# Casting the weights from DRAM to DRAM ahead of use, in a two-layer Mamba-2 and attention kernel

## The reference

```python
# layer 1
x = x + mamba2_mixer(rms_norm(x, a_norm), a_in_proj, ..., a_out_proj)   # SSD, 32 heads, 8 groups
x = x + conv_ffn(x, f_norm[0], f_w_in[0], ..., f_w_down[0])             # gated, width-3 conv
# shared K/V, then layer 2
k, v = split(rms_norm(x, kv_norm) @ w_kv + b_kv)                        # k normed, rotary
q = rotary(rms_norm((rms_norm(x, b_norm) @ w_q + b_q), q_norm))
x = x + sliding_window_sink_attention(q, k, v, sinks) @ w_o + b_o       # window 128
x = x + conv_ffn(x, f_norm[1], f_w_in[1], ..., f_w_down[1])
```

## Time and profile before

| | us |
|---|---|
| median of 3 runs | 2031.58 (2028.68 to 2034.41) |
| the profiled execution, its own time | 2035.03 |
| span of its slowest core, which the profile shows (core 3) | 2034.0 |
| spans of the 8 cores | 2000.2 to 2034.0 |
| PE busy | 1850.5 (91% of the span) |
| DVE, ACT, POOL busy | 1393.1, 1191.9, 204.5 |

### The profile page before, as it was taken

How to read it: one execution, slowest core, us unless ns; L and a number is a source line. 1 busy time by engine, 2 the same in 40 slices (tenths; PEclk the granted TensorE clock), 3 DMA queues, 4 the chain that set the end, 5 groups by cost and what they waited for, 6 DMA issues and landing times.

```text
span 2034.0 us, 34214 instructions; the slowest of 8 cores (2000.2 to 2034.0 us)
## 1 busy us (share of the span) xinstructions
PE 1850.5 (91%) x10024; PEld 823.4 (40%) x10024; DVE 1393.1 (68%) x2384; ACT 1191.9 (59%) x2140; POOL 204.5 (10%) x325
## 2 busy tenths in 40 slices
PE   5787798989888899999999999999999998989999
PEld 3333343434433343444443444444443344433344
DVE  6787477977666675587785776688776656774362
ACT  4688556756767464556577665576476643665330
POOL 1122001122120011000101000000102000020000
PEclk9889899999899999999999999999999999999999
DMA  9879778978556999945432544644423343443344
GB/s 221 195 175 214 188 150 199 211 186 218 144 156 154 221 210 216 280 151 151 156 116 76 162 162 158 203 154 139 148 84 104 128 154 118 145 125 104 118 152 156
DMA packets 111062, 330.59 MB, mean 163 GB/s; under 512 B 14752, under 2 KB 33312, under 8 KB 110880
## 3 DMA queue, kind: packets, MB, share of 16 engines
q1 hardware_dynamic: 95184, 271.56, 40.7%
q0 software_dynamic: 15696, 56.83, 18.1%
HBM read 318.78 MB, written 66.39 MB: 189 GB/s over the span
## 4 chain that ended last, share of the span: by engine, by line
PE 74%; DMA 11%; ACT 5%; issue 5%; DVE 4%; SPq 1%; POOL 0%; DVEq 0%; ACTq 0%; POOLq 0%
PE ps_ps L353 67%; PE ps_ps L366 6%; DMA sb_ring_fw<-w 5%; PE ps_ps L373 2%; DMA sb_ring_mw<-w 2%; DMA w<-sb_ring_fw 1%; DMA al_scr<-sb_AHl 1%; ACT sb_facc L391 1%; DMA sb_SL<-as_scr 1%; DMA sb_facc<-pos 1%; DVE sb_macc L417 1%; SPq L429 1%; DVE sb_uF L406 1%; ACT sb_macc L391 1%; DVE sb_hF L406 0%
## 5 line engine op out<-in xcount | busy, mean ns | idle before, releaser
L353 PE MATMUL ps_ps<-sb_hF,sb_ring_fw 128*128 128x512 bf16 x2464 | 578.8, 382 | 16.0 <-DMA sb_ring_fw<-w 9.7
L353 PE MATMUL ps_ps<-sb_hM,sb_ring_mw 128*128 128x512 bf16 (+1 forms) x1568 | 395.0, 389 | 24.6 <-DVE sb_macc L417 9.1
L353 PE MATMUL ps_ps<-sb_ring_fw,sb_uF 128*128 128x512 bf16 (+1 forms) x1696 | 394.8, 376 | 11.2 <-DVE sb_uF L406 4.6
L353 PEld LDWEIGHTS ps_ps<-sb_hF,sb_ring_fw 128*128 128x128 bf16 x2464 | 235.7, 98 | 298.6 <-issue 37.7
L417 DVE SCALAR_TENSOR_TENSOR sb_facc<-ps_ps,sb_cst,sb_facc 128x511 f32<-128x511 f32 (+2 forms) x400 | 295.9, 745 | 18.3 <-PE ps_ps L353 1.4
L391 ACT ACTIVATE sb_facc<-ps_ps,sb_cst 128x512 f32<-128x512 f32 x213 | 162.7, 766 | 167.8 <-PE ps_ps L353 156.1
L417 DVE SCALAR_TENSOR_TENSOR sb_macc<-ps_ps,sb_cst,sb_macc 128x511 f32<-128x511 f32 (+1 forms) x336 | 247.6, 743 | 12.7 <-PE ps_ps L353 1.4
L353 PEld LDWEIGHTS ps_ps<-sb_ring_fw,sb_uF 128*128 128x128 bf16 x1696 | 158.1, 98 | 202.9 <-issue 42.0
L353 PEld LDWEIGHTS ps_ps<-sb_hM,sb_ring_mw 128*128 128x128 bf16 (+1 forms) x1568 | 149.6, 100 | 205.0 <-issue 56.3
L406 DVE TENSOR_TENSOR sb_xR<-sb_xR,ps_ps 128x512 f32<-128x512 f32 x128 | 86.6, 684 | 122.9 <-PE ps_ps L353 121.4
L353 PE MATMUL ps_ps<-sb_ring_mw,sb_ybuf 128*128 128x512 bf16 (+1 forms) x608 | 156.1, 388 | 15.5 <-DMA sb_ring_mw<-w 10.3
(11 more groups left out here) (219 smaller groups left out, 2309.0 us busy)
## 6 DMA issues: line engine op xcount, KB each, us to landing
sb_ring_fw<-w SPq DMA_DIRECT2D x218, 512.0 KB, 3.8
sb_ring_mw<-w SPq DMA_DIRECT2D x106, 512.0 KB, 5.0
sb_ring_fw<-w POOLq DMA_DIRECT2D x76, 512.0 KB, 9.8
w<-sb_ring_fw SPq DMA_DIRECT2D x76, 512.0 KB, 8.7
sb_ring_mw<-w POOLq DMA_DIRECT2D x32, 512.0 KB, 9.5
w<-sb_ring_mw SPq DMA_DIRECT2D x32, 512.0 KB, 8.0
sb_Er<-er_scr SPq DMA_DIRECT2D x28, 512.0 KB, 8.2
sb_xR<-x SPq DMA_DIRECT2D x16, 512.0 KB, 7.8
```

The costliest lines, as they stand in the source:

```text
L353: return self.add("pe", lambda e: e.matmul(out, lhsT, rhs, start=start, stop=stop), [lhsT, rhs] + ([] if start else [out]), [out], cost=ma ...
```

## The change

The class `Caster` is new. `ahead(tile)` issues, on POOL's queue, DMAs that cast whole tiles from `w32` to `w16`, from DRAM to DRAM, up to a limit that grows with the tile that is in use: 2 tiles ahead at first, one more for every third tile, 12 at most. Each waits for the last matmul that was emitted before it. The rings then load those tiles on SP from `w16` the first time too, after the cast of the tile has landed. The first 11 tiles are still cast on their way into the ring and written back. The gates of the other ring's first four casts go, since these casts are gone.

```diff
+class Caster:
+    def __init__(self, K, w32, w16, first, depth):
+        self.K, self.w32, self.w16 = K, w32, w16
+        self.first, self.depth, self.next = first, depth, first
+        self.gate = None
+        self.done = {}
+
+    def ahead(self, tile):
+        lim = min(NTILE, tile + 1 + min(self.depth, 2 + tile // 3))
+        pe = self.K.ops["pe"]
+        while self.next < lim:
+            j = self.next
+            o = self.K.dma("pool", self.w16[j], self.w32[j], f"cast{j % (self.depth + 2)}")
+            g = pe[-1] if pe and tile else self.gate
+            if g is not None:
+                o.deps.append(g)
+                g.signal = True
+            o.signal = True
+            self.done[j] = o
+            self.next += 1
 class Ring:
...
-            if first:
+            if first and tile < self.caster.first:
                 n = 768 if tile == 0 else SLOT
                 o = self.K.dma("pool", self.buf[:, slot, 0:n], self.w32[tile][:, 0:n], f"{self.name}c{slot}")
...
             else:
+                if tile >= self.caster.next:
+                    self.caster.ahead(tile)
                 n = 768 if tile == 0 else SLOT
                 o = self.K.dma("sp", self.buf[:, slot, 0:n], self.w16[tile][:, 0:n], f"{self.name}{slot}")
                 o.deps.append(self.written[tile])
...
+        if first:
+            self.caster.ahead(tile)
         if first and tile not in self.written:
...
-    written = {}
-    mring = Ring(K, "mw", 4, w32_d, w16_d, written)
-    fring = Ring(K, "fw", 4, w32_d, w16_d, written)
+    caster = Caster(K, w32_d, w16_d, 11, 12)
+    mring = Ring(K, "mw", 4, w32_d, w16_d, caster)
+    fring = Ring(K, "fw", 4, w32_d, w16_d, caster)
...
-                        fring.gate[g - 4] = last
```

More of the change, by code:

```diff
@@ L609, in run, with __init__ @@
         self.drain()
+class Caster:
[17 more added lines that the diff above has]
+            self.next += 1
 class Ring:
-    def __init__(self, K, name, nslot, w32, w16, written):
+    def __init__(self, K, name, nslot, w32, w16, caster):
         self.K = K
@@ L621, in __init__ @@
         self.nslot = nslot
-        self.w32, self.w16, self.written = w32, w16, written
+        self.w32, self.w16, self.caster, self.written = w32, w16, caster, caster.done
         self.buf = K.sb("ring_" + name, [128, nslot, SLOT], BF16)
@@ L844, in build @@
         mring.gate[j] = last
+    caster.gate = last
     K.dma("sp", cf[:], cf_d, "c2")
```

## The result

The change makes the kernel slower: 2152.9 us median of 4 runs (2149.73 to 2158.45) against 2031.32 for the kernel before beside it; ratio 1.0601, 95% interval 1.0573 to 1.0629. The forecast was 1998 us. The profiled execution took 2149.73 us, its span is 2148.7 us (core 3). In the runs `e6_fine` to `e9_late` and `e12_oneplan` to `e14_late12` one die ran slower than the other, in the kernel before too, so their times, and those of two runs compared with them, are the median span of the other die's four cores, marked "die", beside the same median of the kernel before.

The account below looks back on a forecast made before the run. TensorE bounds 1127 to 1471 us; only the first 860 us, where weights first come in, can change. Terms -21 - 3.6 - 5 - 3.7 - 5.7 + 5 = -34 take 2035.0 to 2001, 1998 us as median; range 1975 to 2032.

Parts of the forecast that it names:

- a slot is refilled by a plain load (3.8 us median to landing) and not by a cast (9.8 us): Rings: a freed slot has some 15 us until its next tile is due, so plain loads remove 13.8 us of waits.
- Crowding: Broadcast rows and positions land later beside more DMA work, +5 us; as rival "Crowding eats half", 2021 us, chance 0.20.
- The price of a cast: DMA engines: a DRAM-to-DRAM cast costs 3.4 to 5.0 us of 16 engines, taken as 4 us.
- the bytes' reckoning: DMA engines: for 98 tiles a plain load replaces a write-back of equal bytes, 1.6 us of 16 engines a tile.
- slower: the DMA engines become the bound: Rival, from tile 11 to the last cast: at 6 us a cast the engines are overfull, 2138 us; chance 0.15.
- over 5.3 us a cast: DMA engines: the cast price above which the slower rival's casts cost more than the 34 us won.
- casts may lag up to 12 tiles before anyone waits: Look-ahead of casts: the argument given against the rival that crowding eats half the gain.
- The waits on SP: SP's queue, first two stretches: without write-backs, `al_scr` is issued earlier, -3.6 us, and the positions, -5 us.
- The waits for the mixer ring: Ring waits, taken whole: -3.7 us for the mixer ring, -5.7 us in the out-projection of block 0.
- 18 was expected: SP's waits: the terms 3.6, 5, 3.7 and 5.7 us, 18 us in all, mostly winnable by order alone.
- the two places that I named: SP's queue: the `al_scr` write issued at 289.00 and the positions load at 423.64, both behind write-backs awaiting casts.
- The round of block 1: Second ConvFFN's first pass, in-projection: costs 23.9 us over block 2's round, of which 21 is won, -21 us.

Follow-up runs that it names:

- e6_fine: Changed kernel with each cast issued as four DMAs of 512 columns, pieces of 1 KB: die 2101.1 against 2017.7 us.
- e9_late: Kernel before, only the list schedule told that casts land 6 us later: die 2007.5 against 2017.7 us.
- e12_oneplan: e3_one with the list schedule told that casts land 6 us later: die 2419.9 against 2015.5 us.
- e14_late12: Kernel before, only the list schedule told that casts land 12 us later: die 2028.7 against 2015.5 us.
- e5_small: Kernel before plus 22 unneeded DRAM-to-DRAM casts in 4 KB pieces beside block 2's first ConvFFN: die 2060.1 against 2018.6 us.
- e3_one: Changed kernel, each cast waiting on POOL until the one before it has landed: 2127.45 us, ratio 1.0457 to the kernel before.
- e10_late5: Kernel before, only the list schedule told that casts land 6 us later (e9_late again): 2021.22 us, ratio 0.9932.
- e11_pace: Kernel before with e10_late5's order plus 12 paced DRAM-to-DRAM casts for the second ConvFFN: 2019.11 us, ratio 0.992.
- e4_big: Kernel before plus 22 unneeded DRAM-to-DRAM casts in 32 KB pieces beside block 2's first ConvFFN: die 2056.2 against 2018.6 us.
- e15_onedve: e3_one with POOL's elementwise work moved to DVE: 2134.8 us, ratio 1.0469 to the kernel before.
- e7_dumpfine: Kernel before plus 22 unneeded DRAM-to-DRAM casts in 1 KB pieces beside block 2's first ConvFFN: die 2048.9 against 2017.7 us.

## Why the prediction was wrong

**The step that failed** is "a slot is refilled by a plain load (3.8 us median to landing) and not by a cast (9.8 us)", with "Crowding" beside it, +5 us. 3.8 us is the landing of loads over the whole span, most of them with little beside them on POOL's queue; the same trace had 6.4 us for the mixer ring's 28 plain loads before 520 us, beside casts. I priced crowding by the share of busy DMA time, 1.1 us for a tenth, a slope from rows that stood beside 1.1 to 1.4 casts on the mean. What counts is what is queued on the other queue at that moment. Before, casts were held back by the four slots that they fill; the changed kernel issues up to 12 tiles ahead, with nothing to hold them back but a matmul, and up to 6 are in flight at once. 20.3 us of landing is more than the some 15 us that a ring covers, and PE waited 74.8 us.

The kernel before had the turns the right way round: what was urgent, the cast, stood in POOL's queue and landed in 9.8 us; what stood in SP's, the write-back, took 8.7 us but is read only a block later. The change puts what is urgent into the queue that got 28.5% of the engines' time beside 69.4% (`e5_small`), and look-ahead into the other.

**The price of a cast** was right (4 taken, 3.9 found in the queue), and so was the bytes' reckoning. The rival "slower: the DMA engines become the bound" came within 15 us of the time, 2138 against 2153, by luck: its condition, over 5.3 us a cast, wasn't met, and after the first stretch the share is 0.60 to 0.84. In the first stretch, with 0.93, the trace after looks like it; what tells them apart is `e3_one`, where the same bytes leave PE 2.1 us of waits for the mixer ring there. The argument against the rivals, "casts may lag up to 12 tiles before anyone waits", was true of SP (26 us) and beside the point.

**The waits on SP** for casts (-3.6, -5) were taken away: SP had 105.9 us of them from 256 to 512 us and none from 315 to 608 us after. But `al_scr` then took 20.5 us to land where it took 8.3, and the positions 18.5 where they took 14.7. The waits for the mixer ring (-3.7, -5.7) gave way to longer ones, 74.8 us for it in the first stretch and 11.1 us for the second ring from 608 to 736 us. That some of this can be won is shown by `e10_late5`: about 14 us, where 18 was expected; its gain lies in the mixer of block 0, with a higher clock, more than at the two places that I named.

**The round of block 1** (-21) became +14. The term was also too large by itself: 23.9 us is the difference on core 3. Over the eight cores of the same trace the round of block 1 takes 353.1 to 368.7 us, median 361.0, and the round of block 2 344.1 to 346.2, so the first pass cost the median core some 16 us. With 12 of its 33 tiles loaded plain, `e11_pace` won some 7 us of the round against `e10_late5`, by the eight cores' medians; what all 33 would give isn't shown.

**What is shown and what stays open.** Shown: the casts' queue delays the loads (`e3_one`, 20.3 to 5.2 us; `e4_big`, casts without any user), and with one cast in flight they come too late (`e15_onedve`). At most one in flight costs 4.6%, two 3.9%, up to 12 tiles ahead 6.0%: none of them is free, and a first use now needs two transfers, one after the other (7.5 and 5.2 us in `e3_one`), where one did before. How the some 90 us that `e3_one` loses divide between late casts, products on POOL and a lower clock isn't settled. Whether the urgent loads would fare better on another engine's queue than SP's wasn't tried.

## What to carry to other kernels

A transfer that is moved off the path still stands beside those that stay on it: price a load by its landing beside a full queue, not by a median over the span, and ask which queue holds what is needed next. Look-ahead must be held back by something, but with one transfer in flight at a time its latency can become the bound: in `e3_one` casts end to end were 55% of the chain from 60 to 700 us. Before a first use is split into two transfers, see whether what is to be won isn't to be had by the order of the issues alone. And read a term off several cores: the slowest one's 23.9 us was 16 on the median core.

## What the runs showed of the hardware

- A cast of 1 MB of float32 from DRAM to DRAM landed in 7.5 us (`e3_one`) and cost 2.9 us of 16 engines (`e15_onedve`, an estimate) when only one was in flight, and 3.9 us when they were queued; queued casts landed 5.3 us apart.
- A DMA share of 0.93 moved 168 GB/s with queued casts to DRAM and 209 GB/s with casts into SBUF and write-backs (`e10_late5`).
- Two queues that both had work moved equal counts of packets where the casts' pieces were 4 KB (788 and 768 in 30 us, `e5_small`), less equal ones with 1 KB (1934 and 1708 in 30 us, `e7_dumpfine`) and very unequal ones with 32 KB (229 and 1825 in 55 us, `e4_big`).
- While casts were queued on POOL's queue, an issue on SP took up to 14.0 us (changed kernel, 46 to 315 us); in the kernel before the longest there took 2.4 us.
